# Projections of the second block: from four-byte products to three split products, with low parts prepared a stage earlier

## What is computed

```python
u = rms_norm(h, w_norm_mix[l])
proj = jnp.einsum('btd,dk->btk', u, w_in[l])
conf_a = proj[..., OFF_CONF:OFF_CONF + CONF_WIDTH]
conf_g = proj[..., OFF_CONF + CONF_WIDTH:OFF_Z]
z = proj[..., OFF_Z:OFF_XBC]
xbc = proj[..., OFF_XBC:OFF_DT]
dt_raw = proj[..., OFF_DT:OFF_GATE]
gates = jax.nn.sigmoid(proj[..., OFF_GATE:].astype(jnp.float32)).astype(h.dtype)
c = depthwise_conv(conf_a * jax.nn.sigmoid(conf_g), w_conf_dw[l], b_conf_dw[l])
branch_conf = jnp.einsum('btc,cd->btd', jax.nn.silu(layer_norm(c, ...)), w_conf_out[l])
xbc = jax.nn.silu(depthwise_conv(xbc, w_ssm_conv[l], b_ssm_conv[l]))
y = bidir_ssd(...)
branch_ssm = jnp.einsum('btc,cd->btd', rms_norm(y * jax.nn.silu(z), ...), w_ssm_out[l])
```

## Time and profile before

| what | value |
|---|---|
| median of the runs | 2724.68 us |
| span of the profiled execution | 2721.4 us |
| TensorE busy with matmuls | 2601.4 us, 96% |
| VectorE (DVE) | 1027.4 us, 38% |
| ScalarE (ACT) | 670.7 us, 25% |
| GpSimd (POOL) | 264.2 us, 10% |
| mean granted TensorE clock | 0.977 |
| share of TensorE in the chain that ended last | 88% |
| data moved | 560.77 MB, 206 GB/s |

### The profile page before, as it was taken

The page is one execution under the profiler, slowest core; times in us unless marked ns, Lnnn a source line. Parts: engine busy times, 40 slices in busy tenths (PEclk is TensorE's granted clock), DMA queues, the critical chain, the costliest instruction groups (busy, mean ns, idle before and its releaser), DMA issues.

```text
span 2721.4 us, 39739 instructions
## 1 busy us (share of the span) xinstructions
PE 2601.4 (96%) x17183; PEld 1577.0 (58%) x17183; DVE 1027.4 (38%) x1450; ACT 670.7 (25%) x1195; POOL 264.2 (10%) x267
## 2 busy tenths in 40 slices
PE   8998999999999999999789998999999999999996
PEld 6754478888787787878569983333333333333332
DVE  4336344433356868685886323111111111111111
ACT  3255432222222433332354222000000001000001
POOL 0033000000002112121430000000000000000000
PEclk9999999999999999999889998999999999999998
DMA  5100022212314132323332248999999999999993
GB/s 206 66 27 1 31 95 105 109 65 105 115 41 139 57 125 61 108 76 93 84 125 83 93 193 333 407 396 404 403 396 393 399 396 396 396 394 398 395 404 129
DMA packets 92618, 560.77 MB, mean 206 GB/s; under 512 B 15236, under 2 KB 48004, under 8 KB 59812
## 3 DMA queue, kind: packets, MB, share of 16 engines
q1 hardware_dynamic: 40320, 514.89, 47.9%
q10 hardware_dynamic: 47236, 30.42, 4.1%
q0 software_dynamic: 4896, 12.98, 1.8%
HBM read 541.97 MB, written 16.29 MB: 205 GB/s over the span
## 4 chain that ended last, share of the span: by engine, by line
PE 88%; DVE 7%; ACT 2%; issue 1%; DMA 1%; POOL 0%; ACTq 0%; POOLq 0%; DVEq 0%
PE PS L1069 37%; PE PS L516 16%; PE PS L730 4%; PE PS L971 4%; PE PS L726 4%; PE PS L727 4%; PE PS L976 2%; PE PS L701 2%; DVE H L1876 2%; PE PS L630 1%; PE PS L581 1%; PE PS L577 1%; PE PS L578 1%; PE PS L1059 1%; PE PS L561 1%
## 5 line engine op out<-in xcount | busy, mean ns | idle before, releaser
L516 PE MATMUL PS<-U,ring 128*128 128x264 f32 x2304 | 529.3, 389 | 1.3 <-ACT arena L1348 1.3
L1069 PE MATMUL PS<-expert_ring_low,U 128*32 128x512 f32 x4608 | 509.8, 594 | 0.9 <-DVE U L2118 0.9
L1069 PE MATMUL PS<-expert_ring_high,U 128*32 128x512 f32 x4608 | 504.8, 592 | 0.0
L516 PEld LDWEIGHTS PS<-U,ring 128*128 128x128 f32 x2304 | 437.6, 192 | 82.0 <-issue 8.5
L1069 PEld LDWEIGHTS PS<-expert_ring_high,U 128*32 128x32 f32 x4608 | 148.0, 110 | 336.9 <-issue 335.9
L1069 PEld LDWEIGHTS PS<-expert_ring_low,U 128*32 128x32 f32 x4608 | 146.2, 110 | 332.9 <-issue 331.8
L1876 DVE SCALAR_TENSOR_TENSOR H<-arena,par,H 128x528 f32<-128x528 f32 x240 | 195.4, 858 | 1.4
L2130 DVE TENSOR_TENSOR H<-H,PS 128x512 f32<-128x512 f32 x32 | 22.0, 687 | 439.8 <-PE PS L1069 424.3
L726 PE MATMUL PS<-UX,WF 128*128 128x512 f32 x352 | 137.9, 392 | 0.8 <-DVE UX L1636 0.8
L727 PE MATMUL PS<-UX,WF 128*128 128x512 f32 x352 | 137.0, 389 | 0.0
L1278 ACT ACTIVATE WF<-ring 128x1024 fp32r<-128x1024 f32 (+1 forms) x76 | 72.0, 948 | 245.5 <-PE PS L730 245.5
(11 more groups left out here) (341 smaller groups left out, 3196.9 us busy)
## 6 DMA issues: line engine op xcount, KB each, us to landing
expert_ring_low<-w_experts SPq DMA_DIRECT2D x96, 2048.0 KB, 11.5
expert_ring_high<-w_experts SPq DMA_DIRECT2D x96, 2048.0 KB, 11.4
ring<-w_gu SPq DMA_DIRECT2D x11, 2048.0 KB, 8.0
ring<-ssd_sums ACTq DMA_DIRECT2D x32, 512.0 KB, 7.2
ring<-w_xbc SPq DMA_DIRECT2D x8, 1536.0 KB, 6.5
ring<-w_down SPq DMA_DIRECT2D x8, 1408.0 KB, 6.0
ring<-w_in SPq DMA_DIRECT2D x5, 2048.0 KB, 8.2
ring<-w_conf SPq DMA_DIRECT2D x8, 1024.0 KB, 8.7
```

What stands on the lines that cost most here:

```text
L516: last = nc.tensor.matmul(PS[0:M, banks[i], 0:hi - lo], lhs(k), rhs(k)[:, lo:hi], start=(k == 0), stop=(k == K - 1))
L1069: mm = nc.tensor.matmul(PS[QUAD * t:QUAD * t + QUAD, bank, :], stat(t), move(t), start=start, stop=stop)
```

## The change

The 72 projection tiles are made of three float32r products instead of one f32 product.

- `split_proj` replaces `dense`: per tile 8 x 2 x 3 products of 264 columns, high weights x high input, high x low, low x high. `dt` stays f32.
- The input U is split once: ACT writes UHI (8 copies of 128 x 528), DVE writes ULO over U (8 subtractions), after the `dt` product. The first tile takes its products with ULO last.
- The low parts of the 72 weight tiles are made in the stage of the output product and the feed-forward stage, and stored in DRAM. For each tile GpSimd's queue loads the raw weights (512 KB; three places), ACT makes the high part (`pre_high`, into PSUM banks 6 and 7 except for the first three), DVE the low part (`pre_low`), and GpSimd's queue stores it (512 KB). GpSimd waits for the store of tile q before it issues the load of tile q + 3. `PRE_WO`, `PRE_GATE`, `PRE_DOWN` say how many tiles are made in which step: 3 with the output product, 2 or 3 in each of the 22 steps of gate and up (47), and 4 or 3 in each of the first seven steps of down (22).
- In the scan SyncE loads for each tile the raw weights and the low part (2 x 512 KB) into one of four pairs of places in ring slots 2 and 3, when TensorE is done with the tile four before. ACT makes the high part in place (`tile_high`), up to two tiles ahead of the tile that it takes next (`ready_for`).
- In the feed-forward stage the low parts of the weights are now written in place in the ring, so a slot is free only when TensorE is done with it, not when it is split.
- Buffers of the scan move to ring slots 0 and 1. The first load of `co` waits for the last turned output, the load of `so` 0 and ACT's silu of the convolution branch wait for the last gate tile (`got(act, ("g1", DT - 1))`), because UHI lies where XH is written.
- Semaphores are merged and renamed; the order of the eight first expert loads' places changes with the slots.

The core of the diff:

```diff
@@ pe
-            def proj(tag, w, cols, name):
+            def split_proj(tag, banks):
+                p = PROJ_AT[tag]
+                wh, wl = [proj_split(p, low).rearrange("p (k n) -> p k n", k=DT) for low in range(2)]
+                open_(tag, *banks)
+                def product(w, k, x, start=False, stop=False):
+                    for i, (lo, hi) in enumerate(halves(T2)):
+                        last = nc.tensor.matmul(PS[:, banks[i], 0:HT], w[:, k, :], x[:, k, lo:hi], start=start, stop=stop)
+                    return last
+                pe.wait_ge(S("weights_high"), PROJ_W + p + 1)
+                for k in range(DT):
+                    if p == 0:
+                        pe.wait_ge(S("x_high"), U_X + k + 1)
+                    product(wh, k, UHI, start=k == 0)
+                    if p > 0:
+                        product(wh, k, ULO)
+                pe.wait_ge(S(f"low_in{pair_of(p)}"), 16 * (p // PAIRS + 1))
+                for k in range(DT):
+                    last = product(wl, k, UHI, stop=p > 0 and k == DT - 1)
...
@@ act
+            def pre_high(n):
+                for q in range(pre_turn[0], pre_turn[0] + n):
+                    act.wait_ge(S(f"pre_in{q % STAGE}"), 16 * (q // STAGE + 1))
+                    if q >= len(PRE_WO):
+                        act.wait_ge(S("pre_low"), q)
+                    A(pre_high_place(q), pre_raw(q), ACT.Copy).then_inc(S("pre_high"), 1)
...
             for m in range(FFT):
                 ffn_high(2 * m + 3)
                 if m >= 1:
                     hidden_high(m - 1)
+                    pre_high(1)
                 act.wait_ge(*freed(("ga", m)))
                 A(SQ[:, m % 2, 0:SEQ], SQ[:, m % 2, 0:SEQ], ACT.Silu).then_inc(S("silu_ready"), 1)
                 ffn_high(2 * m + 4)
+                pre_high(PRE_GATE[m] - (m >= 1))
...
+            def tile_high(p):
+                act.wait_ge(S(f"raw_in{pair_of(p)}"), 16 * (p // PAIRS + 1))
+                A(proj_split(p, 0), proj_raw(p), ACT.Copy).then_inc(S("weights_high"), 1)
+            def ready_for(tag):
+                for p in range(tiles_done[0], min(PROJ_AT[tag] + 3, N_PROJ)):
+                    tile_high(p)
...
             inverse_root("lnv", (6, 7), T2)
+            got(act, ("g1", DT - 1))
             for k in range(DT + 1):
@@ dve
+            def pre_low(n):
+                for q in range(pre_turn[0], pre_turn[0] + n):
+                    dve.wait_ge(S("pre_high"), q + 1)
+                    V_.tensor_tensor(PREL[:, q % STAGE, :], pre_raw(q), pre_high_place(q).bitcast(F32), SUB).then_inc(S("pre_low"), 1)
...
+            got(dve, "dt")
+            for k in range(DT):
+                dve.wait_ge(S("x_high"), U_X + k + 1)
+                V_.tensor_tensor(ULO[:, k, :], U[:, k, :], UHI[:, k, :].bitcast(F32), SUB).then_inc(S("x_low"), 1)
@@ pool
+            def pre_load(q):
+                if q >= STAGE:
+                    pool.wait_ge(S(f"pre_out{q % STAGE}"), 16 * (q // STAGE))
+                pool.dma_start(pre_raw(q), inp["w_proj"][q]).then_inc(S(f"pre_in{q % STAGE}"), 16)
+            pool.wait_ge(S("mix_ready"), DIFF_HEADS)
+            for q in range(STAGE):
+                pre_load(q)
+            for q in range(N_PROJ):
+                pool.wait_ge(S("pre_low"), q + 1)
+                pool.dma_start(low_dram[q], PREL[:, q % STAGE, :].bitcast(F32)).then_inc(S(f"pre_out{q % STAGE}"), 16)
+                if q + STAGE < N_PROJ:
+                    pre_load(q + STAGE)
@@ sp
+            def proj_loads():
+                for p in range(N_PROJ):
+                    if p < PAIRS:
+                        slot_free(max(n for n in range(FIRST_TAIL) if slot_of[n] == 2 + pair_of(p) // 2))
+                    else:
+                        got(sp, PROJ[p - PAIRS])
+                    sp.dma_start(proj_raw(p), inp["w_proj"][p]).then_inc(S(f"raw_in{pair_of(p)}"), 16)
+                    sp.wait_ge(S(f"pre_out{p % STAGE}"), 16 * (p // STAGE + 1))
+                    sp.dma_start(proj_split(p, 1).bitcast(F32), low_dram[p]).then_inc(S(f"low_in{pair_of(p)}"), 16)
```

More of the change, by code:

```diff
@@ L71 @@
 TBUF = 4
-TAIL = ("co", "so", "out")
 CONF_AHEAD = 2
@@ L86 @@
 TAPS_BEFORE = [min(n for n, (u, j) in enumerate(TAP_ORDER) if u == t) for t in range(DT)] + [len(TAP_ORDER)]
+PROJ = [("xb", 0, 0), ("xb", 0, 1), ("ca", 0), ("cg", 0), ("ca", 1), ("cg", 1)]
+for _g in range(GROUPS):
+    PROJ += [("xb", _g, t) for t in range(2 if _g == 0 else 1, 6)]
+    PROJ += [gate for gate, at in zip(GATE_OF, GATES_AT) if at == (_g, "conv")]
+    PROJ += [("zt", 4 * _g), ("zt", 4 * _g + 1)]
+    PROJ += [gate for gate, at in zip(GATE_OF, GATES_AT) if at == (_g, "late")]
+    PROJ += [("zt", 4 * _g + 2), ("zt", 4 * _g + 3)]
+    for _c in range(5):
+        PROJ += [gate for gate, at in zip(GATE_OF, GATES_AT) if at == (_g, _c)]
+        if _g < GROUPS - 1:
+            PROJ.append((("ca", "cg")[_c % 2], 2 * _g + CONF_AHEAD + _c // 2) if _c < 4 else ("xb", _g + 1, 0))
+PROJ += [("g1", m) for m in range(4, DT)]
+PROJ_AT = {tag: n for n, tag in enumerate(PROJ)}
+N_PROJ = len(PROJ)
+STAGE = 3
+PAIRS = 4
+PRE_WO = (1, 2, 3)
+PRE_GATE = [2 + (m in (5, 11, 17)) for m in range(FFT)]
+PRE_DOWN = [4, 3, 3, 3, 3, 3, 3, 0]
+assert len(PRE_WO) + sum(PRE_GATE) + sum(PRE_DOWN) == N_PROJ
+FFN_W = 24
+PROJ_W = FFN_W + 2 * FFT + 32
+TAIL_W = PROJ_W + N_PROJ
+TAIL_LOW = PROJ_W
+FFN_USED, TAIL_USED = 6, 30
+GX_X = 2 * DT
+U_X = GX_X + FFT
+CONF_X, Y_X, MERGED_X = U_X + DT, U_X + 2 * DT, U_X + 4 * DT
 BIG = 1e30
@@ L272, in program @@
         SGB = RS
-        FR = [[ring[:, 2 * b + d, 3072:4096].rearrange("p (h n) -> p h n", h=GH) for d in range(2)]
-              for b in range(2)]
+        FR = [[beside[:, FR_AT + GH * P * (2 * b + d):FR_AT + GH * P * (2 * b + d + 1)].rearrange("p (h n) -> p h n", h=GH)
+               for d in range(2)] for b in range(2)]
         MG = arena[:, 0:DT * T2].rearrange("p (a n) -> p a n", a=DT)
@@ L369, in program @@
             landed[name] = count[slot_of[n]]
-        AFTER_FFN = [loads[min(n for n in range(where[("dt",)], N_DENSE) if slot_of[n] == b)][0] for b in (0, 1)]
+        FIRST_TAIL = where["co", 0]
         last_read = {}
@@ L416, in raw, with split_high, split_low @@
             return slot(name, part)[:, k0:k0 + n, m * P:m * P + P]
-        def split(which, p):
+        def split_high(p):
             n = pieces[p][3]
-            return WF[:, which, p % FBUF, 0:n * P].rearrange("p (k n) -> p k n", k=n)
+            return WF[:, p % FBUF, 0:n * P].rearrange("p (k n) -> p k n", k=n)
+        def split_low(p):
+            name, part, k0, n, m = pieces[p]
+            at, k, w = loads[where[name]][1][part]
+            v = RINGF[:, slot_of[where[name]] - 2, at:at + k * w].rearrange("p (k n) -> p k n", k=k)
+            return v[:, k0:k0 + n, m * P:m * P + P]
         piece_used = []
@@ L790, in conf @@
             def conf(u, part):
-                arrived(("conf", u))
-                proj((("ca", "cg")[part], u), slot(("conf", u), part), slice(0, P), ("conf", u))
+                proj((("ca", "cg")[part], u))
             def gates(at):
@@ L960, in split_dense @@
                 open_((kind, m), *banks)
-                for kh, (high, low, sem, base) in enumerate(parts):
+                for kh, (high, low, base) in enumerate(parts):
                     p = TPIECE[kind, m, kh]
@@ L1305, in _ @@
                         ffn_high(p)
+                    pre_high(PRE_DOWN[m])
                 if m >= 1:
@@ L1508, in tail_split_high @@
                     tail_used(act, p - TBUF)
-                A(tail_high(p), tail_raw(ring, p), ACT.Copy).then_inc(S("tw_high"), 1)
-            got(act, last_read[loads[max(j for j in range(N_DENSE) if slot_of[j] == RING - 1)][0]])
+                A(tail_high(p), tail_raw(ring, p), ACT.Copy).then_inc(S("weights_high"), 1)
+            got(act, ("g1", 5))
             for p in range(TBUF):
@@ L2395, in _ @@
             sp.wait_ge(S("stored"), 64)
-FLAT = {"down": lambda b, kh: 2 * b + kh, "dt": lambda: 0, "g1_last": lambda b: b}
-for _kind in ("xbc", "z"):
-    FLAT[_kind] = lambda g, i: 2 * g + i
-for _kind in ("in", "wo", "gu", "conf", "g1", "co", "g2", "so", "out"):
+FLAT = {"down": lambda b, kh: 2 * b + kh}
+for _kind in ("in", "wo", "gu", "co", "so", "out"):
     FLAT[_kind] = lambda b: b
```

279 lines of the change are left out of this document (147 added, 132 removed).

## The result

The changed kernel is slower: 2815.79 us, median of four runs from 2812.15 to 2821.09, against 2724.69 us (2724.12 to 2724.99) for the kernel before beside it. The ratio is 1.0335, 95% interval 1.0323 to 1.0348. The forecast was 2666, range 2640 to 2712. The profiled execution has a span of 2811.0 us against 2721.4, so 89.6 us were added.

The account below looks back on a forecast made before the run. TensorE, busy for 96% of the span, was taken as the bound. Of 91 us saved on tiles 69 were left; less 5 (clock), 3.7 (silu), 1 (feed-forward) and 0.5 (input split), 59 us gave 2666 us, range 2640 to 2712.

Parts of the forecast that it names:

- The store's landing time: GpSimd's loop in the feed-forward stage: a 3.9 us store makes a 4.7 us turn, within the 5.17 us available.
- Rival 1: GpSimd's loop bounds the feed-forward stage, costing 69 x (turn - 5.17) us, a loss from 6.0 us; chance 0.18.
- The estimate of 3.2 us: GpSimd's 512 KB store by the skill page's fit: 3.2 us, a loop of 4.0 us and no loss.
- The tiles: All 72 projection tiles: 5.85 instead of 7.12 us each, 91 us saved if TensorE sets the pace everywhere.
- clock: Line 913 in the back stretches: longer waits for M1 bring TensorE's lower clock, costing 5 us.
- (a): Back stretch up to M1: VectorE can give up only 1.8 us; 10 us lost in three groups, 2 in the last.
- (b): Chunk stretch: VectorE's step without idle time gains nothing, the other gives its 1.27 us a tile; 4 us lost.
- Rival 2: Scan: ScalarE's copies and late decays fall on VectorE's string, so chunk and back stretches gain nothing; 2693 us, chance 0.20.
- the last four tiles: End of the scan: these tiles only fill the time of the layer norm, so 5 us of saving is lost.
- the silu: Behind the last gate tile: ACT's silu for `co` now waits for that tile, making the first `co` tile 3.7 us late.

Follow-up runs that it names:

- e1: Changed kernel with GpSimd's loop reordered: each load waits for the store before the one just issued, so two stores can overlap; 2715.98 us, 0.9972 of the kernel before.
- e7: Against e1: low parts of 32 tiles not prepared but made in the scan by GpSimd's subtraction; 2749.37 us, 1.0078 of the kernel before.
- e2: Changed kernel with low-part stores on ScalarE's queue, each behind its wait for the next load; 2725.9 us, 1.0008 of the kernel before.
- e6: Against e2: each store issued ahead of the wait for the next load, copies and subtractions placed evenly in down; 2698.51 us, 0.9896 of the kernel before.
- e11: Against e6: all eight silus ahead of ScalarE's wait for the last gate tile, VectorE's eight scalings ahead of its first low part; 2695.37 us, 0.9884.
- e12: The kernel of e6 run again unchanged, on the chip of the run beside it; 2705.67 us, 0.9926 of the kernel before.

## Why the prediction was wrong

**The store's landing time, the step that failed.** The forecast took 3.9 us for a store and 4.7 for a turn, against 5.17 needed, and put 1 us with a range of 0 to 15. The store took 5.4 us (median; 9 to 10 beside a 2 MB load), a turn 6.8 us. Rival 1 named this, with the mechanism, the point from which it decides (6.0 us) and the price; by its formula a turn of 6.83 us gives 115 us where the stage lost 135.5. It had 0.18, too little: the bounds ran from 3.5 to 15.1 us, the limit of 5.17 stood near the lower end, and the row that spoke for a loss was the only store from GpSimd in the trace.

The forecast priced the store as a transfer by itself, after rows of 3.8 and 2.7 us, and counted one issue in a turn where there are two. It counted 200 GB/s of new traffic, but used it only for the gate and up loads. For a store by itself the price was more than enough: four stores of the changed kernel go out with no other transfer issued in the 3 us ahead of them, and they land in 2.8 to 2.9 us. But nearly every store goes out 0.5 us behind the load that the loop has just issued, of the same size, and none of these landed in less than 5.0. The chain shows one of each kind, the second with its load ahead:

```profile
715.36 2.85 DMA projection_low_parts<-PREL
...
718.49 0.52 POOL arena L2306
719.01 5.28 DMA projection_low_parts<-PREL
```

So it is less the mean traffic, 220 GB/s from 380 to 600 us, than what the loop itself puts ahead of each store: e1 moves 293 GB/s in that stretch, but each store goes out ahead of the load, and the stores land in 4.3 us (median); in e7, in the same order and at 190 GB/s, in 2.9. This is read from the traces; no run keeps the serial wait and parts the two transfers.

**The mean against the burst.** The cost was a mean turn against a mean need. The transfers beside a 2 MB load took 10 us, and three places could not cover that: the reordered loop, whose short turn is 3.9 us a piece, still came to 5.2.

**The estimate of 3.2 us.** It was worked out from the page "DMA: Bandwidth & Descriptors" of the Trainium skill (Anatomy of one DMA), which fits a single DMA. For a store alone it is above the 2.8 us here, and for the stores behind a load it is far below the 5.4. The rule of the Trainium skill's page "SBUF — State Buffer" (SBUF: two separate sides), that GpSimd cannot write descriptors beside certain VectorE operations, was not seen to decide anything: ScalarE's queue gave 3.4 us in e2, but 6.4 in e6, and GpSimd's gave 2.9 in e7. No run isolates it.

**The tiles.** 5.85 us a tile was right, and so was the conv part as TensorE's: the 46 tiles outside the chunk parts and ahead of the last four were worth 58.4 us, and 57.7 arrived.

**Back stretch, chunks, clock: right in mechanism, too small in size.** For the 22 tiles of the chunk parts, 28 us, the forecast took 17 for VectorE and 5 for the clock and kept 6; measured is a loss of 2.9 (68.7 to 68.1 and the like, the first 67.0 to 70.1), 9 us less. More than half of the 9 is in (a). VectorE's string from the start of the back stretch to M1 was to give up the 1.8 us in which it waited for TensorE. It gave up 0.45 in the second group: 33.72 us before, 33.27 in the changed kernel, although it no longer waits for TensorE. The waits were filled by two of VectorE's own operations that got longer. Before:

```profile
992.87 0.54 DVE L1873 TENSOR_SCALAR H<-arena,par 128x528 f32<-128x528 f32 x1
```

and 0.69 us for line 1922 behind it; in the changed kernel, with GpSimd's operation of the same moment:

```profile
1102.91 1.27 DVE L1973 TENSOR_SCALAR H<-arena,par 128x528 f32<-128x528 f32 x1
1104.10 1.53 DVE L2022 TENSOR_TENSOR arena<-arena,ring 128x512 f32<-128x512 f32 x1
```

```profile
1102.57 1.31 POOL L2325 TENSOR_TENSOR arena<-arena,ring 128x512 f32<-128x512 f32 x1 [2.87 <-PE PS L907]
```

TensorE's state product is ready 1.2 us earlier in the string and releases GpSimd, whose operations now run beside these two; before, GpSimd's began only together with line 1922, at 993.78. That they cause the lengthening was not tested here; e7 shows the same on a larger scale. It makes 1.3 to 1.5 us in each of the four groups. The first half of the chunk part, from the first CB to the first YD product, got 2.1 us longer in the second group (17.8 to 19.9) and 8.5 in all four, where the forecast comes to some 3 in all.

Line 957 then waits 6.06 us for M1 and takes 3.67 us at the lower clock, where 4.8 and 1.7 more than 2.00 were forecast:

```profile
1128.91 3.67 PE L957 MATMUL PS<-arena 128*128 128x64 f32 x16 [6.06 <-DVE arena L2038]
```

The rest of the 9 us is in (b), the second half: 12.60 us with 1.69 us idle was taken to give up all 1.27 us a tile. The four second halves went from 212.6 to 207.2 us, 5.4 less where the forecast comes to some 9, and in the other traces of this scan they take 209.4 to 213.5. Rival 2 had this picture of the chunk parts, though it put ScalarE's copies and the late decays at their root; its sum left 56 us of tiles, and 57.7 arrived outside them.

**The last tiles and the tail.** Forecast for the last four tiles and the silu together: a loss of 3.6 us. Measured: 5.3, and 3.5 more behind the first `co` product, of which the forecast had nothing. e11 finds 6.4 us there by the order of silus and low parts.

In sum the scan was put at a gain of 59.8 us (69 - 5 - 3.7 - 0.5), measured 45.9, and without preparation 39.5 by the medians; the stage ahead of it was put at -1, measured -135.5.

## What to carry to other kernels

Where one in-order queue stores a piece and then waits for that landing before the next load, the landing time is the period of everything behind it; with the wait for the store before instead, the same 72 loads and 72 stores cost 100 us less here. Size a transfer that must keep pace by what is issued beside it after the change, not by a median from another stretch, and give the rival that stands on it the chance that the width of its bounds asks for. A gain in one engine's work counts only in stretches where the next engine has room: here 46 of 72 tiles.

## What the runs showed of the hardware

A 512 KB store with no transfer right ahead of it takes 2.8 to 2.9 us from GpSimd's queue (after) and 2.6 from ScalarE's (e2, e6, e12); 0.5 us behind a load of the same size it takes 5.0 at least, 5.4 in the median (after); and loads and stores alike take about 10 us when most of a 2 MB transfer of another queue runs beside them (e1, e2). GpSimd's 128x1024 subtraction takes 2.5 us and stops a two-input VectorE operation for 2.1 of them (e7). And a wait can cost TensorE more than its length: in the changed kernel line 957 takes 3.67 us behind a wait of 6.06 us and 1.89 in the next chunk, where it does not wait. The mean granted clock is 0.92 and 0.85 in the two stretches of the feed-forward stage in which TensorE waits for 52 and 47 us, and 1.00 in the conv parts, where it does not.
